# SSD scans of an encoder trunk: decay differences on ScalarE by Relu, directions added on VectorE, z's banks read earlier

## What is computed

```python
a_cs = jnp.cumsum((dt * a).reshape(b, c, t, g, e), axis=2)      # t = 128 positions in a chunk
seg = a_cs[:, :, :, None] - a_cs[:, :, None, :]
decay = jnp.exp(jnp.where(lower, seg, -jnp.inf))
cb = jnp.einsum('bclgn,bcsgn->bclsg', Cc, Bc)
y_diag = jnp.einsum('bclsge,bcsgep->bclgep', cb[..., None] * decay, X)   # X = xs * dt
...
y = y_fwd + y_bwd + d_skip.astype(f32)[:, None] * xs
y = y.reshape(...) * jax.nn.silu(z)
```

## Time and profile before

| | us |
|---|---|
| median of 3 runs | 1648.07 |
| lowest, highest | 1647.79, 1648.29 |
| the profiled execution | 1648.22 |
| its span, first to last instruction | 1646.4 |
| TensorE busy in the span | 1624.9 |
| VectorE, ScalarE, GpSimd busy | 967.1, 682.7, 674.3 |

### The profile page before, as it was taken

The page is one execution under the profiler, slowest core; times in us unless marked ns, Lnnn a source line. Parts: engine busy times, 40 slices in busy tenths (PEclk is TensorE's granted clock), DMA queues, the critical chain, the costliest instruction groups (busy, mean ns, idle before and its releaser), DMA issues.

```text
span 1646.4 us, 19523 instructions
## 1 busy us (share of the span) xinstructions
PE 1624.9 (99%) x7480; PEld 1280.2 (78%) x7480; DVE 967.1 (59%) x1532; ACT 682.7 (41%) x948; POOL 674.3 (41%) x339
## 2 busy tenths in 40 slices
PE   7999999999999999999999999999999999999999
PEld 5776778777878888888877777787878788888887
DVE  4578869787755445522227778798877554544000
ACT  5556652335343333332244665524444433333221
POOL 3432222333445555554443322223234555555443
PEclk9999999999999999999999999999999999999999
DMA  5532135442223232223324221444422223232323
GB/s 168 132 104 83 52 115 146 134 147 92 90 90 103 90 94 99 90 94 96 93 90 128 87 74 64 131 151 127 146 93 90 91 92 100 90 97 92 96 93 109
DMA packets 57372, 170.88 MB, mean 104 GB/s; under 512 B 5984, under 2 KB 11872, under 8 KB 57280
## 3 DMA queue, kind: packets, MB, share of 16 engines
q1 hardware_dynamic: 56896, 168.88, 33.0%
q0 software_dynamic: 384, 0.75, 0.4%
HBM read 166.24 MB, written 3.38 MB: 103 GB/s over the span
## 4 chain that ended last, share of the span: by engine, by line
PE 91%; DMA 2%; issue 2%; POOL 2%; ACT 1%; DVE 1%; SPq 0%; DVEq 0%; POOLq 0%; ACTq 0%
PE banks L1169 27%; PE banks L1171 26%; PE banks L1170 26%; PE banks L1256 2%; PE banks L1247 2%; PE banks L1267 2%; DMA sb_w_raw<-w_out 2%; PE banks L1319 1%; PE banks L1332 1%; PE banks L1227 1%; PE banks L1346 1%; POOL sb_xc L476 0%; DMA sb_x_stream<-x_t 0%; PE banks L1303 0%; DVE sb_h_lo L817 0%
## 5 line engine op out<-in xcount | busy, mean ns | idle before, releaser
L436 POOL TENSOR_TENSOR sb_w_lo<-sb_w_raw,sb_w_hi 128x1024 fp32r<-128x1024 f32 x200 | 482.5, 2413 | 622.0 <-ACT sb_w_hi L531 622.0
L1169 PE MATMUL banks<-sb_h_hi,sb_w_hi 128*128 128x512 f32 x1344 | 547.6, 407 | 13.2 <-POOL sb_w_lo L436 11.9
L531 ACT ACTIVATE sb_w_hi<-sb_w_raw 128x1024 fp32r<-128x1024 f32 x256 | 270.9, 1058 | 695.2 <-PE banks L1171 674.2
L1171 PE MATMUL banks<-sb_h_hi,sb_w_lo 128*128 128x512 f32 x1344 | 530.8, 395 | 0.0
L1170 PE MATMUL banks<-sb_h_lo,sb_w_hi 128*128 128x512 f32 x1344 | 530.5, 395 | 0.0
L1169 PEld LDWEIGHTS banks<-sb_h_hi,sb_w_hi 128*128 128x128 f32 x1344 | 253.4, 189 | 90.7 <-issue 30.1
L1170 PEld LDWEIGHTS banks<-sb_h_lo,sb_w_hi 128*128 128x128 f32 x1344 | 253.6, 189 | 62.3 <-issue 6.5
L1171 PEld LDWEIGHTS banks<-sb_h_hi,sb_w_lo 128*128 128x128 f32 x1344 | 253.3, 188 | 59.4
L1134 DVE TENSOR_TENSOR banks<-banks,sb_rstd 128x512 f32<-128x512 f32 x88 | 61.5, 699 | 145.2 <-PE banks L1171 135.7
L1169 PE MATMUL banks<-sb_ff_hi,sb_w_hi 128*128 128x512 f32 x352 | 138.9, 395 | 0.0
L1170 PE MATMUL banks<-sb_ff_lo,sb_w_hi 128*128 128x512 f32 x352 | 138.9, 395 | 0.0
(11 more groups left out here) (204 smaller groups left out, 2231.8 us busy)
## 6 DMA issues: line engine op xcount, KB each, us to landing
sb_w_raw<-w_in SPq DMA_DIRECT2D x88, 512.0 KB, 3.6
sb_w_raw<-w_up SPq DMA_DIRECT2D x88, 512.0 KB, 3.5
sb_w_raw<-w_out SPq DMA_DIRECT2D x32, 512.0 KB, 3.6
sb_w_raw<-w_down SPq DMA_DIRECT2D x32, 512.0 KB, 3.4
sb_e<-sum_rows SPq DMA_DIRECT2D x16, 512.0 KB, 6.0
sb_bias_t<-bias_rows SPq DMA_DIRECT2D x16, 448.0 KB, 6.2
sb_exp_cs<-sum_rows SPq DMA_DIRECT2D x32, 192.0 KB
sb_w_raw<-w_down SPq DMA_DIRECT2D x16, 384.0 KB, 3.0
```

The lines of the kernel that those rows point to most:

```text
L436: g.tensor_tensor(WLO[:, n % 2, :], W[:, n % 2, :], WHI[:, n % 2, :].bitcast(F32), ALU.subtract).then_inc(w_lo.handle, 1)
L531: sc.activation(WHI[:, n % 2, :], W[:, n % 2, :], ACT.Copy).then_inc(w_hi.handle, 1)
L1169: mm(out, whi, hhi, start=start, stop=False)
L1171: return mm(out, wlo, hhi, start=False, stop=stop)
```

## The change

Four things change, in code that both layers run.

- **Differences and cap on ScalarE.** `seg` goes. `head_exp(h)` waits for the head's rows itself, and for each direction and chunk replaces the row value r by Relu(A - r), where A is the column of `AS`. Then one exponential over 128x1024 takes exp(CAP - value), with `CAP` a column as its bias operand. `AS` is made with CAP added, CAP being the largest of a partition's logarithms of dt, by one new `tensor_reduce` in slot 1. So what is exponentiated is capped at CAP instead of 80.
- **Directions on VectorE, for every head.** `add_directions` leaves GpSimd, where it ran for even heads, and runs on VectorE for all 16, behind `low_after` of the slot in which the head is weighed.
- **`within` issues two matmuls a chunk, not three**, since the odd head's directions are already added. It waits for the odd head's sum.
- **z's banks are read earlier**: the block for `z` stands ahead of `weigh` and `low_after`, where that for `o1` stands.

```diff
+    CAP = sb("log_caps", [P, 1])
...
         def head_exp(h):
-            act.wait_ge(*seg_done.at(h + 1))
-            sc.activation(head_e(h), head_e(h), ACT.Exp).then_inc(e_done.handle, 1)
+            if h == 0:
+                act.wait_ge(*cs_col.at(1))
+            act.wait_ge(*rows_landed[h % 4].at(16 * (h // 4 + 1)))
+
+            for d in (0, 1):
+                for c in range(QT):
+                    at, col = slice(P * c, P * c + P), column(d, h)
+                    ins = sc.activation(head_e(h)[:, d, at], head_e(h)[:, d, at], ACT.Relu, bias=AS[:, c, col:col + 1], scale=-1.0)
+            ins.then_inc(gap_done.handle, 1)
+            act.wait_ge(*gap_done.at(h + 1))
+            sc.activation(head_e(h), head_e(h), ACT.Exp, bias=CAP[:, 0:1], scale=-1.0).then_inc(e_done.handle, 1)
...
-        def seg(h):
-            dve.wait_ge(*rows_landed[h % 4].at(16 * (h // 4 + 1)))
-
-            for d in range(2):
-                for c in range(QT):
-                    at = slice(P * c, P * c + P)
-                    ins = v.tensor_scalar(head_e(h)[:, d, at], head_e(h)[:, d, at], AS[:, c, column(d, h):column(d, h) + 1], 80.0,
-                                          ALU.subtract, ALU.min)
-            ins.then_inc(seg_done.handle, 1)
...
+        def add_directions(h):
+
+            dve.wait_ge(*g_done.at(h + 1))
+            v.tensor_tensor(head_e(h)[:, 0, :], head_e(h)[:, 0, :], head_e(h)[:, 1, :], ALU.add).then_inc(gs_done.handle, 1)
...
+                    step(v.tensor_reduce(CAP[:, :], SM[:, 2, :], mybir.AxisListType.X, ALU.max))
                     for d in range(2):
...
-                if s in SEG_AT:
-                    seg(SEG_AT[s])
...
+                if kind == "z":
+                    dve.wait_ge(*w_used.at(POS[kind, i] + 1))
+                    if i < 4:
+                        dve.wait_ge(*sc_lo.at(4))
+                    else:
+                        dve.wait_ge(*y_comb.at(i - 3))
+                    v.tensor_tensor(Z[:, i % 4, :], bank(b), RSTD, ALU.mult).then_inc(evac[b].handle, 1)
...
                     weigh(WEIGH_AT[s])
                 low_after(kind, i)
+                if s in WEIGH_AT:
+                    add_directions(WEIGH_AT[s])
...
-            pe.wait_ge(*gs_done.at(t + 1))
-            pe.wait_ge(*g_done.at(2 * t + 2))
+            pe.wait_ge(*gs_done.at(2 * t + 2))
...
-                for h, d in ((2 * t, 0), (2 * t + 1, 0), (2 * t + 1, 1)):
+                for h in (2 * t, 2 * t + 1):
                     half = 64 * (h % 2)
                     ins = mm(BANK[half:half + 64, 6 + t % 2, P * c:P * c + P], XT[:, c, 64 * (h % 8):64 * (h % 8) + 64],
-                             head_e(h)[:, d, P * c:P * c + P], start=d == 0, stop=d == h % 2)
+                             head_e(h)[:, 0, P * c:P * c + P], start=True, stop=True)
```

More of the change, by code:

```diff
@@ L279, in build_trunk @@
     cb_mm, cb_done, xs_done, st_mm, sin_done = sem("cb_mm", 2), sem("cb_done", 4), sem("xs_done", 12), sem("st_mm", 12), sem("sin_done", 8)
-    seg_done, e_done, g_done, y_mm = (
-        sem(n, SSD_HEADS) for n in ("seg_done", "e_done", "g_done", "y_mm"))
-    gs_done = sem("gs_done", SSD_HEADS // 2)
+    gap_done, e_done, g_done, y_mm = (
+        sem(n, SSD_HEADS) for n in ("gap_done", "e_done", "g_done", "y_mm"))
+    gs_done = sem("gs_done", SSD_HEADS)
     yo_mm, y_read, t_read, z_copied, y_comb = (sem(n, 8) for n in ("yo_mm", "y_read", "t_read", "z_copied", "y_comb"))
@@ L497, in _ @@
                             scale_states(6 * grp + 2 * (s - GROUP_AT[grp]) + j)
-                if s in WEIGH_AT and WEIGH_AT[s] % 2 == 0:
-                    add_directions(WEIGH_AT[s])
                 if s in PAIR_AT:
@@ L1042, in _ @@
                     dve.wait_ge(*lndt_done.at(1))
+                    step(v.tensor_reduce(CAP[:, :], SM[:, 2, :], mybir.AxisListType.X, ALU.max))
                     for d in range(2):
-                        step(v.tensor_tensor(AS[:, :, DIR * d:DIR * d + DIR], BANK[:, 3, P * d:P * d + P].rearrange("p (c n) -> p c n", n=DIR),
-                                             SM[:, 2, :].rearrange("p (c n) -> p c n", n=64)[:, :, DIR * d:DIR * d + DIR], ALU.subtract))
-                    dve.sem_inc(cs_col.handle, 1)
-                if s in SEG_AT:
-                    seg(SEG_AT[s])
+                        ins = v.scalar_tensor_tensor(AS[:, :, DIR * d:DIR * d + DIR], BANK[:, 3, P * d:P * d + P].rearrange("p (c n) -> p c n", n=DIR),
+                                                     CAP[:, 0:1], SM[:, 2, :].rearrange("p (c n) -> p c n", n=64)[:, :, DIR * d:DIR * d + DIR],
+                                                     ALU.add, ALU.subtract)
+                    ins.then_inc(cs_col.handle, 1)
                 for grp in range(SSD_GROUPS):
@@ L1089, in _ @@
                         dve.wait_ge(*sca_done.at(2 * t + 1 + tp // 2))
-                if kind == "z":
-                    dve.wait_ge(*w_used.at(POS[kind, i] + 1))
-                    if i < 4:
-                        dve.wait_ge(*sc_lo.at(4))
-                    else:
-                        dve.wait_ge(*y_comb.at(i - 3))
-                    v.tensor_tensor(Z[:, i % 4, :], bank(b), RSTD, ALU.mult).then_inc(evac[b].handle, 1)
                 if 21 <= s < 25:
@@ L1329, in within @@
             for c in range(QT):
-                for h, d in ((2 * t, 0), (2 * t + 1, 0), (2 * t + 1, 1)):
+                for h in (2 * t, 2 * t + 1):
                     half = 64 * (h % 2)
                     ins = mm(BANK[half:half + 64, 6 + t % 2, P * c:P * c + P], XT[:, c, 64 * (h % 8):64 * (h % 8) + 64],
-                             head_e(h)[:, d, P * c:P * c + P], start=d == 0, stop=d == h % 2)
-                    if c == QT - 1 and d == h % 2:
+                             head_e(h)[:, 0, P * c:P * c + P], start=True, stop=True)
+                    if c == QT - 1:
                         ins.then_inc(y_mm.handle, 1)
```

3 lines of the change are left out of this document (removed).

## The result

| | before | after |
|---|---|---|
| median, us | 1647.99 | 1651.54 |
| lowest, highest (17 runs each) | 1647.42, 1648.98 | 1649.78, 1653.63 |
| the profiled execution | 1648.2 | 1649.9 |

The ratio is 1.0021, interval 1.0015 to 1.0028: 3.6 us slower, where I had forecast 18.4 us faster and a range that ended at 1640. The change took 14.1 us of matmuls out of TensorE's list, as it should. Then it gave everything back in three places: every large matmul became slower, since a new column of 4 bytes had moved the activation buffers; waits for VectorE's sum appeared at pairs 3 and 7; and one of these waits cost TensorE its clock for a moment.

The account below looks back on a forecast made before the run. TensorE, busy 99% of the span, was taken as the bound, so the kernel is as long as its list. Terms: -15.2 - 4.6 + 0.4 + 0.9 = -18.5 us from 1648.2, giving 1629.7; range 1626 to 1640.

Parts of the forecast that it names:

- What TensorE no longer issues: At `within` (line 1332), 8 records instead of 16 set a pair's length: 0.95 us saved a pair, 15.2 us in all.
- Half-wide matmuls are limited by issue: Rival at `within`: the 0.079 us a record is an issue limit, saving 10.1 instead of 15.2, 1634.8 us; chance 0.12.
- The new `tensor_reduce` and slot 1's two instructions: On VectorE in slot 1: covered by a 2.52 us wait for ScalarE; uncovered they would cost under 1 us a layer.
- Waits that go: TensorE's waits at pairs 3 and 7 (3.2 us) and for z's banks (1.4 us) vanish: 4.6 us saved.
- 8 x 0.364 = 2.9 us: VectorE's price for one head's differences, taken as what made it late for `within` at pairs 3 and 7.
- What VectorE pays: The odd head's sum behind `low_after` makes `within` late in slot 5: 0.45 us a layer, 0.9 in all, bounds 0 and 1.6.
- In later pairs the sum is ready over 1 us early: For pairs after slot 5's, VectorE's odd-head sum was claimed ready over 1 us early.
- What the transfers pay: ScalarE asks for heads' rows earlier; only head 5's and head 7's come after it is free; no cost counted.
- I count nothing: The transfers' term in the sum: slot 9's high part ends about 0.3 us before it would bind, so no cost.
- Nothing moves: Rival: TensorE's saving is waited for at the next weights, transfers setting the pace of pair slots; chance 0.04.
- What ScalarE pays: A head takes 3.6 us instead of 1.05, hidden except around slots 20 to 23: 0.4 us in all.
- Both rivals on ScalarE: Relu make weights late, 1634.1 us, up to 1638, chance 0.19; or ScalarE becomes the bound, 1666 us, chance 0.05.

Follow-up runs that it names:

- the change with the regions in place: The changed kernel with CAP put in unused bytes behind neg_max, so no buffer behind it moves, against before: 1645.45 us, ratio 0.9984.
- sum-first kernel: The changed kernel with CAP in neg_max's unused bytes, plus VectorE's add_directions ahead of low_after instead of behind it, against before: 1636.33 us, ratio 0.9933.

## Why the prediction was wrong, point by point

- **What TensorE no longer issues: right.** 0.95 us a pair was forecast and (1.90 - 1.02) = 0.88 came, 14.1 us for 16 pairs instead of 15.2. The halves run side by side, so the rival "Half-wide matmuls are limited by issue" falls.
- **What was not in the sum: the place.** The step on the new column ("The new `tensor_reduce` and slot 1's two instructions") priced its instructions and not its bytes. The bytes cost 6.1 us (1651.54 - 1645.45). Without it the result would still have been 1645.45, above my range.
- **Waits that go: right as far as the weighing goes.** z's waits are gone. At pair 3 the weighing ends at 301.38 instead of 302.95, just as TensorE gets there, and at pair 7 it ends 2 us ahead of TensorE. What is waited for in these slots now is the low part and the sum behind it. The price was misread on the way: "8 x 0.364 = 2.9 us" adds up instructions that overlap. The row of 8 took 1.66 us at pair 3, 4.52 at pair 7 and 37.5 / 16 = 2.3 in the mean of the earlier trace rows. In all VectorE has 56.5 / 32 = 1.8 us a head less to do, for "about 2".
- **What VectorE pays: the failed step** is "In later pairs the sum is ready over 1 us early". I worked it out for slot 5 alone, where it is nearly right: `within` of pair 0 starts 0.2 us late in a layer (1.64 us behind `from_states` instead of 1.43), for 0.45 forecast. At pair 3 the sum is 2.6 to 3.0 us late, the low part ahead of it stretched to 2.04 us as in the earlier trace rows. At pair 7 it is 1.2 to 1.4 us late, the low part at 1.58 us and the sum itself at 1.75, for 0.76 to 1.00 forecast; what stretches it there was not tested.
- **What the transfers pay: the second failed step**, "I count nothing". I had held the late load of the earlier trace rows only against the tile that needs it. It never was late for that tile. A load like it was late for VectorE, which waits for it in order with the sum behind. At pair 3 of layer 0 the wait can be added up: VectorE is done with the work that hangs on the load at 298.83 in both kernels. From there to what `within` waits for it was 302.95 - 298.83 = 4.1 us before and is 303.94 - 298.83 = 5.1 now, TensorE gets there at 301.38 instead of 302.51, and it waited 0.54 before: 1.0 + 1.1 + 0.5 = 2.6. Of the rivals, "Nothing moves" comes nearest, since transfers help to set the pace at pair 3 and in half of the wait at pair 7. But they do it through the sum and not at the next weights, and not in the other pair slots.
- **What ScalarE pays: right.** A head takes 3.5 us for 3.6 forecast: the row of 8 Relu 2.44 us (388 ns each, 0.29 apart), the exponential 1.15. The Trainium skill ("ScalarE: Activation LUTs", section "What ACT_TABLE_LOAD costs") has back-to-back ACTIVATEs overlap by about 93 ns, and 388 - 93 = 295 agrees. Slots 20 to 23 wait 0.2 us in all. Both rivals on ScalarE fall: weights were made late by the load and by VectorE's order, not by the Relu.

Together, for the profiled executions of before and of the change with the regions in place (1648.2 and 1643.0, 5.2 us less): 14.1 us of matmuls went. TensorE's listed waits grew from 18.2 us to 24.3, these three rows of the second kernel the most:

```profile
PE banks L1331 <- DVE sb_squares L920: 9.0, 4, 3.1
...
PE banks L1331 <- DVE sb_e L920: 1.3, 4, 0.4
PE banks L1218 <- POOL sb_sq_ssd L452: 1.1, 1, 1.1
```

The fall of the clock at pair 3 of layer 1 made the pair 0.71 us and the next tile 0.91 us longer, 1.6 us. That makes -14.1 + 6.1 + 1.6 = -6.4, and 1.2 us stay unplaced. In after itself the waits sum to only 21.5 us, at the slower pitch. My reading, not tested, is that a slower TensorE gets to a late load later and waits less.

And for the forecast of 1629.7 itself: the place makes up 6.1 us of the miss of 21.8, the order of low part and sum 9.1. The sum-first kernel with the regions in place is still 6.6 us above the forecast. Of these, 1.1 us are what the matmuls saved less than forecast, and 4.1 are waits of TensorE: 19.0 us where the forecast left 18.2 - 4.6 + 1.3 = 14.9. 1.4 us stay open.

## What to carry to other kernels

When work is put behind another instruction on an in-order engine, take the start of the chain from what that instruction waits for, the transfer included, and not from the engine's own load; then ask whether it could stand ahead. Compare the start-to-start time of a matmul that a change doesn't touch: if it moved, a buffer moved, and one spare buffer tells what that costs. The distance between the two operands of the main matmul is worth a trial by itself; here it gave 25.9 us, and the change as written 2.5 to 5.4 at equal distance. And when time moves with no change in the list of a busy TensorE, look at the granted clock of each run.

## What the runs showed of the hardware

**The distance of two operands.** For fp32 matmuls of 512 columns the time from start to start was 0.2325 us at 148.5 times 256 bytes between `w_hi` and `h_hi`, 0.2343 with 32 bytes more, 0.2333 with 64, and 0.2275 at 149 and at 150 times 256. So a multiple of 128 or of 64 isn't enough. Of the matmuls between the same two buffers, 192 stream the weights and hold the activations, and they follow the distance in another way: 0.233 us at 148.5 times 256 and with 32 bytes more, 0.229 with 64, 0.228 at 149 times 256. Attention's products with the probabilities, both of whose operands were moved, didn't change. Other distances weren't tried.

**The clock after a wait.** At pair 3 of layer 1 TensorE stood idle for 3.04 us. Windows around it (us, busy and count of PE, PEld, DVE, ACT and POOL, clock, DMA share, GB/s):

```profile
1114.00:1118.00 4.00, 0.96 (x12) 0.77 (x13) 4.00 (x4) 1.46 (x2) 1.26 (x1) 1.00 0.08 33
1118.00:1121.00 3.00, 3.00 (x20) 2.38 (x16) 2.89 (x5) 0.23 (x1) 0.00 (x0) 0.50 0.91 278
1121.00:1124.00 3.00, 3.00 (x14) 2.40 (x13) 1.01 (x2) 0.00 (x0) 1.00 (x1) 0.93 0.89 249
```

The clock fell from 2.4 to 1.2 GHz for about 3 us, after work had begun again. Timeline of TensorE there:

```profile
1117.70 0.32 PE L1331 MATMUL banks<-sb_e_third,sb_x_tok 128*64 128x128 f32 x1 [3.04 <-DVE sb_squares L920]
...
1118.38 0.42 PE L1331 MATMUL banks<-sb_e_third,sb_x_tok 128*64 128x128 f32 x1
...
1120.40 0.63 PE L1171 MATMUL banks<-sb_h_hi,sb_w_lo 128*128 128x512 f32 x1
1120.82 0.63 PE L1169 MATMUL banks<-sb_h_hi,sb_w_hi 128*128 128x512 f32 x1
```

Narrow records take 0.42 us instead of 0.27, and wide ones start 0.42 apart instead of 0.23. The pair takes 1.68 us instead of 1.02, and the 24 starts of the next tile 6.39 instead of 5.49: 1.6 us beside the wait itself. At pair 3 of layer 0, after 2.61 us idle, the clock stayed at 1.00:

```profile
303.00:307.00 4.00, 3.01 (x25) 2.48 (x26) 3.96 (x6) 1.06 (x1) 0.00 (x0) 1.00 0.61 203
```

The length of the wait alone doesn't decide it. In the changed kernel with the regions in place TensorE stood idle for 3.08 us at pair 3 of layer 0 and for 3.09 in layer 1, and the clock fell in layer 1 alone. With the differences left on VectorE the clock fell after 2.22 us idle at pair 3 of both layers, and stayed after 3.41 us at pair 7 of layer 1. How much clock a run loses goes with its time. Before's runs lie 1.6 us apart, and every one whose clock was read has 1.000. Of the 17 of after, eight have a mean granted clock of 0.999 (seven at 1649.78 to 1650.68 us, one at 1653.12), eight 0.998 (1651.24 to 1653.32) and one 0.997 (1653.63). So every run of the changed kernel, with its longer waits, loses a little clock, and most of its wider spread goes with how much.
